# Last block of a three-part transformer kernel: where its head norms, bias tiles and compression stand among the projection blocks and heads

## The reference

```
def second_block(x, c, rel_bias, ada_w, ...):
    u = rms_norm_2(h, norm1_g[layer]) * (1 + scale1) + shift1
    z = u @ w_in[layer]
    q_a, kc, vc, ksl, vsl, kwn, vwn, g_a, q_b, k_b, v_b, m_a, m_b = jnp.split(z, split_at, axis=-1)
    q_a = rms_norm_2(q_a.reshape(B, S, NSA_HEADS, HEAD_DIM), q_norm_g[layer])...
    k_cmp = rms_norm_2(compress_blocks(kc, cmp_pos, cmp_k_w1, cmp_k_w2), k_norm_g[layer, 0])
    v_cmp = compress_blocks(vc, cmp_pos, cmp_v_w1, cmp_v_w2)
    k_slc = rms_norm_2(ksl, k_norm_g[layer, 1])
    k_win = rms_norm_2(kwn, k_norm_g[layer, 2])
    g_nsa = jax.nn.sigmoid(g_a)
    y_a = nsa_attention(q_a, k_cmp, v_cmp, k_slc, vsl, k_win, vwn, g_nsa, rel_bias) @ w_up_nsa
    y_b = stick_breaking_attention(q_b, k_b, v_b) @ w_up_sb
    mixed = (jax.nn.sigmoid(m_a) * y_a + jax.nn.sigmoid(m_b) * y_b) @ w_out[layer]
    h = h + gate1 * mixed
```

## Time and profile before

| | us |
|---|---|
| median of 3 runs | 2562.81 |
| lowest and highest run | 2561.25, 2563.6 |
| the profiled execution, its own time | 2561.44 |
| its span in the trace | 2559.7 |
| PE busy, share of the span | 2472.3, 97% |
| DVE busy | 1695.5, 66% |
| ACT busy | 1302.7, 51% |
| mean granted PE clock | 0.977 |

### The profile page before, as it was taken

The page is one execution under the profiler, slowest core; times in us unless marked ns, Lnnn a source line. Parts: engine busy times, 40 slices in busy tenths (PEclk is TensorE's granted clock), DMA queues, the critical chain, the costliest instruction groups (busy, mean ns, idle before and its releaser), DMA issues.

```text
span 2559.7 us, 41603 instructions
## 1 busy us (share of the span) xinstructions
PE 2472.3 (97%) x16654; PEld 2266.6 (89%) x16654; DVE 1695.5 (66%) x3136; ACT 1302.7 (51%) x2461; POOL 435.6 (17%) x389
## 2 busy tenths in 40 slices
PE   7799999999999999999999999999999997998999
PEld 7689999999988888787999999998888886888999
DVE  4834799777777777656489977775555553536654
ACT  4234444566644444465454466665454543555543
POOL 4600000188600000000000028850000000002000
PEclk8899999999999999999999999999999998999999
DMA  6103455433377777641345543345555563223442
GB/s 238 67 33 132 141 182 183 172 132 129 128 270 258 261 266 259 227 178 45 121 166 186 184 158 133 133 141 207 196 191 195 193 237 128 87 91 132 164 166 83
DMA packets 93199, 421.81 MB, mean 165 GB/s; under 512 B 10297, under 2 KB 12881, under 8 KB 85073
## 3 DMA queue, kind: packets, MB, share of 16 engines
q1 hardware_dynamic: 93008, 419.16, 46.4%
HBM read 415.96 MB, written 3.16 MB: 164 GB/s over the span
## 4 chain that ended last, share of the span: by engine, by line
PE 92%; DVE 3%; ACT 2%; issue 1%; DMA 1%; POOL 1%; SPq 0%; POOLq 0%; DVEq 0%; ACTq 0%
PE PS L170 91%; DVE mem L191 1%; ACT mem L181 1%; ACT r_sh L181 1%; DVE hT L199 1%; PE PS L173 1%; DMA mem<-in_ev_in 0%; DVE r_sl L191 0%; POOL r_hlo L191 0%; POOL hT L191 0%; DMA mem<-in_v 0%; DMA mem<-in_ada 0%; DVE mem L202 0%; ACT xT L181 0%; ACT small L181 0%
## 5 line engine op out<-in xcount | busy, mean ns | idle before, releaser
L191 DVE TENSOR_TENSOR r_sl<-mem,r_sh 128x1024 fp32r<-128x1024 f32 (+2 forms) x750 | 892.6, 1190 | 623.9 <-ACT r_sh L181 623.1
L181 ACT ACTIVATE r_sh<-mem 128x1024 fp32r<-128x1024 f32 (+2 forms) x750 | 768.0, 1024 | 488.8 <-PE PS L170 433.9
L170 PE MATMUL PS<-r_hhi,r_sh 128*128 128x256 f32 x3280 | 838.0, 292 | 25.1 <-ACT r_hhi L181 19.8
L170 PE MATMUL PS<-r_hlo,r_sh 128*128 128x256 f32 (+1 forms) x3152 | 794.2, 289 | 7.4 <-DVE r_hlo L191 2.8
L170 PEld LDWEIGHTS PS<-r_hhi,r_sh 128*128 128x128 f32 x3280 | 639.0, 195 | 34.4 <-issue 28.2
L170 PEld LDWEIGHTS PS<-r_hlo,r_sh 128*128 128x128 f32 (+1 forms) x3152 | 612.8, 194 | 16.9 <-DVE r_hlo L191 6.6
L170 PE MATMUL PS<-r_hhi,r_sl 128*128 128x256 f32 x3280 | 470.5, 286 | 0.0
L181 ACT ACTIVATE mem<-PS 128x256 f32<-128x256 f32 (+14 forms) x633 | 219.0, 353 | 463.3 <-PE PS L170 459.7
L196 POOL TENSOR_SCALAR xT<-cst,mem 128x128 f32<-128x128 f32 x256 | 327.8, 1293 | 617.9 <-ACT mem L181 555.9
L170 PEld LDWEIGHTS PS<-r_hhi,r_sl 128*128 128x128 f32 x3280 | 431.5, 195 | 0.5 <-DVE r_sl L191 0.2
L170 PE MATMUL PS<-r_sh,r_ch 128*128 128x512 f32 x1024 | 276.5, 391 | 1.6 <-ACT r_sh L181 1.6
(11 more groups left out here) (136 smaller groups left out, 2113.7 us busy)
## 6 DMA issues: line engine op xcount, KB each, us to landing
mem<-in_u SPq DMA_DIRECT2D x256, 512.0 KB, 3.2
mem<-in_v SPq DMA_DIRECT2D x256, 512.0 KB, 4.0
mem<-in_w SPq DMA_DIRECT2D x16, 2048.0 KB, 7.9
mem<-in_ada SPq DMA_DIRECT2D x48, 512.0 KB, 4.6
mem<-in_in SPq DMA_DIRECT2D x9, 2048.0 KB, 7.9
mem<-in_wq SPq DMA_DIRECT2D x8, 2048.0 KB, 7.8
mem<-in_od_in SPq DMA_DIRECT2D x6, 2048.0 KB, 10.4
mem<-in_ev_in SPq DMA_DIRECT2D x5, 2048.0 KB, 11.1
```

Of the source, the lines that this page charges most:

```text
L170: return self.did(self.e and self.e.matmul(out, lhsT, rhs, start=start, stop=stop, skip_group_check=skip))
L181: return self.did(self.e and self.e.activation(out, in_, func, **kw))
L191: return self.did(self.e and self.e.tensor_tensor(out, a, b, op))
```

## The change

It moves work within the last block, on PE, ACT and DVE; SP's order stays.

- Compression, head norms and bias tiles move in among the blocks of N0 and N2. PE makes one flip product behind each block of N0, the key norm's product (both key sets in one of 512 columns) behind the second, the first compression ahead of N2, the q_a norm and the second compression behind N2's second part. Banks are dealt anew (`FIRST_BANK`), N2 uses banks 4 and 5.
- The rest of the compression is cut into steps of the head loop (`compressed(i)` on PE and on DVE, the same steps inline on ACT): `kvc` at turn 0, `kc_ss` at turn 1, `lc` at turn 2, softmax at turns 3 and 4, `PcTp` at turn 5. They share bank 5. Two waits of PE on its own products are new (`rows64`, at turns 0 and 2).
- No FILL block stands before the head loop: 19 are made in it and 9 in the stick-breaking loop (before: 7, 19 and 2).
- The gate's sigmoid becomes exp(-x) on ACT and an add and a reciprocal on DVE.
- The compressed values of a group are added to the output at its last item, in one go for both key heads.

```diff
-            head_norm_ac(ac, qaf, 1024, sq, r, (2, 3), "qa", [("out", N0[3])])
-            head_norm_ac(ac, kvTf[:, 512:768], 256, sq[:, 1024:1280], r[:, 1024:1280], (4,), "k1", [("out", N1[3])])
-            head_norm_ac(ac, kvTf[:, 768:1024], 256, sq[:, 1280:1536], r[:, 1280:1536], (5,), "k2", [("out", N1[3])])
...
+                elif i == 10:
+                    for a in range(2):
+                        ac.wait_ge("cmp", a)
+                        ac.activation(hid15[0:15, 128 * a:128 * a + 128], PS[0:15, 3 - a, 0:128], ACT.Silu).then_inc("cmpS", a)
...
+                if i == 1:
+                    ac.wait_ge("kc", 0)
+                    ac.activation(cm[:, 0:15], kcT[:, 0:15], ACT.Square).then_inc("kc_sq", 0)
+                    ac.wait_ge("kc_ss", 0)
...
-            block_R(pe, N2, (2, 3), ("out", N2[3]))
...
+            for i, n in enumerate(N1 + N0):
+                block_T(pe, n, FIRST_BANK[i], ("out", n), after_norm=None if i else 4)
+                if i >= 4:
+                    flip(i - 4)
+                if i == 5:
+                    pe.wait_ge("hn_sq", "k12")
+                    bank_wait(pe, 2)
+                    pe.matmul(PS[:, 2, :], C("bd64"), sq[:, 1024:1536], True, True).then_inc("hn_ss", "k12", 0)
+                    emptied[2] = ("hn_ln", "k12", 0)
+            compress(0)
+            for u, _ in enumerate(parts_R(pe, N2, (4, 5), ("out", N2[3]))):
+                if u == 1:
+                    head_norm_pe(pe, 1024, sq, (0, 1), "qa")
+                    compress(1)
...
+            def compressed(i):
+
+                if i == 0:
+                    pe.wait_ge("hrep", 0)
+                    bank_wait(pe, 5)
+                    for hk in range(2):
+                        rows = slice(64 * hk, 64 * hk + 64)
+                        pe.matmul(PS[rows, 5, 0:15], P("kw2")[rows, :], hid[rows, 0:15], True, True)
+                        m = pe.matmul(PS[:, 5, 64 + 64 * hk:128 + 64 * hk], hrep[rows, :], P("vw2")[rows, :], True, True)
+                        if hk == 0:
+                            pe.wait_ge(*m.then_inc("rows64"))
...
+                elif i == 1:
+                    bank_wait(pe, 5)
+                    pe.wait_ge("kc_sq", 0)
...
-            for _ in range(5):
-                next(fill)
-            pe.wait_ge("Pc", 0)
...
+                compressed(i)
```

More of the change, by code:

```diff
@@ L1813, in last @@
         NEXT = FILL + UPS_N + OUT2 + W1[0:1]
+        FIRST = N1 + N0 + N2
+        FIRST_BANK = (0, 1, 2, 3, 4, 5, 0, 1)
         gs1, gs2 = take(8), take(8)
@@ L1921, in last_ac @@
             norm_ac(ac, 4, lambda c: mod[:, c:c + 1])
[L1922 to L1925, removed]
+            ns = FIRST + FILL
+            hi(ac, ns[1])
+            for i, n in enumerate(FIRST):
                 if i < 8:
                     ac.wait_ge("wdone", n)
-                    ac.activation(kvT[:, i, :] if i < 4 else qa[:, i - 4, :], PS[:, i % 6, 0:256], COPY).then_inc("out", n)
+                    ac.activation(kvT[:, i, :] if i < 4 else qa[:, i - 4, :], PS[:, FIRST_BANK[i], 0:256], COPY).then_inc("out", n)
@@ L1929, in last_ac @@
                 elif i == 11:
+                    ac.ready(LNEXP)
                     ac.wait_ge("wdone", n)
                     for t in range(2):
[L1932 to L1936, removed]
@@ L1946, in last_ac @@
[L1946 to L1949, removed]
-            for _ in range(5):
[L1951 to L1956, removed]
+                        ac.activation(vnsa[:, t, :], PS[:, 4 + t, 0:256], COPY)
@@ L2056, in last_ve, with blocks @@
             norm_ve(ve, 4, N1[0], lambda c: gs1[:, c:c + 1], lambda c: mod[:, c:c + 1])
[L2057 to L2060, removed]
+            ve.wait_ge(*ve.memset(hid, 0.0).then_inc("dveC"))
+            ve.wait_ge(*ve.memset(hrep, 0.0).then_inc("dveC"))
+            ve.wait_ge(*ve.memset(vblk, 0.0).then_inc("dveC"))
+            def blocks(a):
+                ve.wait_ge("out", N1[a])
                 kview = kvT[:, a, :].rearrange("p (c j) -> p j c", j=16)
@@ L2135, in last_ve @@
-            ve.wait_ge(*d.then_inc("dveC"))
-            ve.tensor_tensor(P3, L3, cm[:, 16:32].rearrange("p (n o) -> p n o", o=1).broadcast_to([128, 16, 15]), MUL).then_inc("Pc", 0)
+            ve.wait_ge(*ve.memset(Pc, 0.0).then_inc("dveC"))
+            lo(ve, FILL[0])
+            for a in range(2):
+                ve.wait_ge("hidT", a)
+                ve.tensor_copy(hv[:, a, 0:15], PS[:, a, 0:15]).then_inc("hid", a)
+            ve.wait_ge("hid", 1)
+            ve.tensor_copy(hrep.rearrange("p (g c) -> p g c", g=4)[:, :, 0:16],
+                           hid[:, 16:32].rearrange("p (o c) -> p o c", o=1).broadcast_to([128, 4, 16])).then_inc("hrep", 0)
@@ L2137, in last_ve @@
+            ve.wait_ge(*gates)
             for i in range(19):
@@ L2156, in last_ve @@
                     stick_low(i // 2 - 2)
+            for _ in fill:
+                pass
             stick_low(3)
@@ L2237, in last_pe @@
             fill = fill_pe(pe)
-            next(fill)
-            pe.wait_ge("hrep", 0)
-            for hk in range(2):
-                rows = slice(64 * hk, 64 * hk + 64)
-                bank_wait(pe, hk)
-                bank_wait(pe, 2 + hk)
-                pe.matmul(PS[rows, hk, 0:15], P("kw2")[rows, :], hid[rows, 0:15], True, True)
-                pe.matmul(PS[:, 2 + hk, 0:64], hrep[rows, :], P("vw2")[rows, :], True, True).then_inc("kvc", hk)
-                emptied[hk] = emptied[2 + hk] = ("kc_v", hk)
```

237 lines of the change are left out of this document (133 added, 104 removed).

## The result

The changed kernel takes **2543.51 us** (median of four runs, 2540.70 to 2545.89) against 2563.20 for the kernel before on the same chip (four runs, 2561.25 to 2564.03). The ratio is 0.9924 [0.9907, 0.9941], 19.7 us off, interval 15 to 24. The forecast was 2544.2 and a net 17.9. The profiled execution took 2540.70, its span is 2538.9.

What follows compares the result with a forecast made beforehand. PE was taken to bound the kernel (92% of the span), with waits and half clock in the last block's serial part. 27.4 gone less 9.5 left gives 17.9 us off 2561.44, 2543.5, plus 0.7: 2544.2 us, range 2538 to 2552.5.

Steps and rivals of the forecast that it cites:

- rows64: PE's two new waits on its own products, turns 0 and 2: 0.4 us lost in all, range 0 to 0.7.
- Rival D: The stretch's end hangs on something other than PE, so moved blocks only lengthen the loops: 2562 us, chance 0.02.
- What goes, 27.4: Last block before the loops: waiting and half-clock loss removed, piece length less dense work, six pieces summing to 27.4 us.
- the silu wait: PE idles ahead of hidT while ACT makes a high half, a table load and two silus: 1.3 us, new.
- its piece: 2150.25 to 2159.70, 9.45 us for lc (2.8) and a block (2.88): 3.8 us gone, all of it clock.
- What covers the moved work: Flips, DVE additions, ACT squares and logs fit beside blocks, q_a norm beside the second compression; no load becomes late.
- What is left, 9.5: New losses in the changed kernel: 1.3 silu, 2.8 turn 1, 0.4 PE's own products, 5.0 clock, together 9.5 us.
- kc_sq: Turn 1: PE waits for ACT's square, placed after item 1's exps, a copy and a high half; 2.8 us, new.
- Clock: Half clock after the idle at turn 1 and at lc in turn 2: 5.0 us lost, bounds 0 and 7.6.
- The hidden steps: Turns 2 to 5: kcn ready 0.6 us before PE needs it, Pc and PcT 4 us before; no PE waits.
- Rival B: Late kcn, Pc or PcT hold PE up in their turns, 8 us given back: 2552.2 us, chance 0.18.
- rival A: PE stays at 2.4 GHz through the first turns despite waits; 5.0 us better, 2539.2 us, chance 0.20.

Runs made afterwards that it cites:

- The first part alone: Changed kernel with only norms, flips and first half of compression moved among the blocks, the rest serial as before; 2551.33 us, ratio 0.9957 to the kernel before.
- the edit that removes it: Changed kernel, but ACT squares the compressed keys at the head of turn 1, ahead of exps and high half; 2538.68 us, ratio 0.9915 to the kernel before.
- the two others: The changed kernel run again unaltered in two later groups; medians 2544.10 and 2544.38 us, ratios 0.9927 and 0.9923 to the kernel before.
- the silus first: Changed kernel, but ACT makes the compression's two silus ahead of FILL[0]'s high half; 2539.69 us, ratio 0.9908 to the kernel before.
- that last kernel: Changed kernel with silus first, the compressed keys' square early, and DVE's hidT copies ahead of FILL[0]'s low half; 2537.69 us, ratio 0.9900 to the kernel before.

## Why the prediction was right

- **What is bound by what.** Right: the gain came from PE's stretch alone, a block moved into the stick-breaking loop costs 2.86 there (6.02 a turn in place of 3.16), and the first up projection came at 2283.27 against "near 2286". Rival D is out. The part behind the stretch, 255.7 and 255.6, shows no loss there, as far as one pair of traces can.
- **What goes, 27.4.** It holds as a sum: the 20.6 us gained in the profiled execution and the new losses of 7.7 below make 28.3. The account has 25.3 of it as waits and clock of the kernel before. Two pieces were mis-sized. N2's parts gave 0.6 and not 1.0: they took 7.20 us, and take 6.6 without the silu wait. And I had priced `lc` at 2.8 us, since 23 passes "start" in a slice of 2 us. They don't: 23 records touch the slice, three of them of the block before, and towards its end the two halves of `lc`, which use different rows of PE, run beside each other. In this half microsecond 11 records touch the slice, where 6 do with one half alone (after, 2147.50 to 2148.00):

```profile
2151.50:2152.00 0.50, 0.50 (x11) 0.50 (x10) 0.22 (x1) 0.18 (x1) 0.00 (x0) 1.00 0.00 0
```

  The rate of one half alone, at clock 1.00, stands in PE's weight loads after:

```profile
2146.99 1.86 PEld L170 LDWEIGHTS PS<-mem 64*128 64x128 f32 x16 [0.17 <-issue]
2149.00 2.30 PEld L170 LDWEIGHTS PS<-mem 64*128 64x128 f32 x19 [0.16 <-PE PS L170]
```

  The 16 passes of a half take 1.86 us, the steps between their starts are 0.11. In the kernel before, the second half began at 2151.6, ahead of the last pass of the first at 2151.9, so `lc` was 3.2 us of dense work there. Of the 9.45 us of its piece 3.4 were clock, half of the spell from 2152.8 to 2159.6, not 3.8: the term was 0.4 too high. With both, 26.6 in place of 27.4.
- **What covers the moved work.** Right: no wait of PE from N1 to N2's end besides the two for r_hlo, 1.1 us, right behind the first product, which the kernel before has too, and the squares, logs and flips cost nothing that shows. The first part alone gave 10.9, where its pieces, 1.0 + 9.4 less the silu wait of 1.3, say 9.1.
- **What is left, 9.5.** The silu wait 1.33 for 1.3. `kc_sq` 2.13 for 2.8: same cause, shown by the edit that removes it; the DVE chain ahead of it was a little shorter than my hand order. `rows64` cost about 0.8 for 0.4, a little above its bound of 0.7. Its idle time is small (0.16 for the loads in the rows above), but the halves of `lc` no longer run beside each other. Before, the second half started 0.33 us ahead of the first's last pass, now 0.32 behind it (2148.68 and 2149.00), 0.65 in all; at turn 0 the step between the two halves grew by 0.13. Before, the halves of `lc` wrote to two banks; now they share bank 5. Clock 3.4 in the profiled execution for 5.0, and 6.8 and 5.1 in the two others, mean 5.1: the term was right for the kernel, and the first trace drew a low one. That makes 7.7 of 9.5 in this execution. 26.6 less 7.7 is 18.9 of the 20.6 measured there; the last 1.7 I cannot place, and they go with the 2 us that the account leaves in the kernel before.
- **The hidden steps.** `kcn` had 0.6 us to spare by my order, and PE came to `lc` without a wait: DVE's last step for it starts at 2144.46 in the trace and takes 0.23, `lc` starts at 2146.99. The margin is 2.3 us, not 0.6: the half clock of 2142 to 2145.5 held PE up by 1.7 and not DVE. `Pc` and `PcT` made no wait either. Rival B did not come.
- **The clock.** I took rival A, a clock that holds, as one chance in five because a row of before had 0.50 behind 2.19 us of waiting and 0.69 in `lc` without idle time. Both came again: 0.55 from 2142 behind a wait of 2.13, and a spell at `lc`, in it or within 1.6 us behind its end, in all fourteen traces. With all waits at 0.2 us the first is gone and the second not, so idle time is not the only cause; that it is one rests on the traces with and without the wait, and the 2.05 us with the silus first show that such a wait can also leave the clock at 1.00. The rule of the Trainium skill ("TensorE: Matmul & The Clock Gate", Part 1) that long idle gaps bring the clock down does not account for that last kernel: its trace has 0.50 at 2150, with one wait of 0.2 us in the 50 us ahead and PE busy for all of that slice. There the measurement decides.

The forecast and its main reasons held. That it came within 1 us is luck: `lc`, `rows64`, `kc_sq` and the clock of the first trace were each off by 0.4 to 1.6 us, partly against each other, and single runs of this kernel lie 5 us apart. What I had not seen is how the clock is spread between executions of one kernel, in the stretch and in code that was not touched, and what a wait on PE's own product costs.

## What to carry to other kernels

Steps with small work between engines belong beside work that PE has anyway, and it is their order on the helping engine, not their cost, that decides whether PE waits: 0.2 to 0.4 us of silus (with a table load of 1.28), a square or two copies, placed behind a high or a low half, cost PE 1.3, 2.1 and 0.6. Put such an operation ahead of the long one whenever its input is ready, and look for the next in line, since the first wait removed uncovers the second. Account for a stretch as idle time plus about half of the half-clock time in which PE is busy: a wait is paid twice where the clock falls behind it, and here a row of tiny products was followed by half clock with no wait at all. Compare several executions before a gain of 1 or 2 us is put down to an edit.

## What the runs showed of the hardware

- The same kernel has half-clock spells of 6.8, 13.6 and 10.2 us in the same stretch in three executions, with the same waits to 0.1 us. Half of the difference is 3.4 us, so below that one trace of each doesn't tell two versions apart.
- A float32 pass of 64 rows and 15 columns comes every 0.11 us with PEld busy throughout, nearly as far apart as the 256-column products of the blocks (0.12). So the columns don't set the step there; that the loads do is likely and wasn't tried apart.
- Alternating with a block's products, one product of 64 rows costs 0.29 us more than in a row of its own kind.
- Products on different 64 rows of PE, into different banks, ran beside each other: before, 4 passes of the second half of `lc` started ahead of 2152.0, the first of them 0.33 us ahead of the first half's last. With a wait between the halves that is lost, 0.65 us.
- A wait of 2.13 us had half clock behind it in all four traces that have one; a wait of 2.05 us and one of 2.04 had not.
- A spell of half clock came within `lc` or behind it in all fourteen traces, with no idle time and no load needed, 3.4 to 10.2 us long, 13.7 with twice the products and 20.5 with them spread. What of these products brings it, their few columns, their 64 rows or the idle array between passes, wasn't tried apart.
